# First block of a three-part transformer kernel: queries and keys projected early, all rotary turns on VectorE, scores of two heads in alternating halves of the array

## What is computed

```
p = u @ w_in                                  # u: normed, modulated x; (512, 2816)
q, k = rms_norm per head(q), (k);  q = rope_2d(q);  k = rope_2d(k)      # pairs within 16 + 16 columns
k_c, v_c = the same k and v columns of the context, k_c normed, not turned
o = softmax(q k_all^T / 8) v_all              # k_all, v_all: 256 context + 512 own tokens
attn = o * silu(p[za])
y = conv(a * sigmoid(g)), width 31, depthwise over 512 channels;  layer norm, silu, @ w_pw, * silu(p[zc])
h = x + gate * (concat(attn, y) @ w_out)
mod = silu(c) @ w_mod                         # the shifts, scales and gates of all blocks
```

## Time and profile before

| what | before |
|---|---|
| median of 3 runs (1949.14 to 1953.25) | 1950.08 us |
| the profiled execution: its time, its span | 1951.19 us, 1949.5 us |
| granted TensorE clock, mean of the profiled execution | 0.936 |
| TensorE busy | 1723.2 us, 88% of the span |
| VectorE busy | 1026.1 us, 53% |
| ScalarE busy | 653.0 us, 33% |
| GpSimd busy | 591.1 us, 30% |
| DMA | 187.14 MB, mean 96 GB/s |

### The profile page before, as it was taken

One profiled execution on the slowest core, in us unless ns is written; L12 is line 12 of the kernel. 1 busy time (PEld: TensorE's weight loads), 2 busy tenths in 40 slices (PEclk: granted clock), 3 DMA queues, 4 the chain that ended last, 5 costly groups with the idle time before them and its releaser, 6 DMA issues.

```text
span 1949.5 us, 23737 instructions
## 1 busy us (share of the span) xinstructions
PE 1723.2 (88%) x9380; PEld 1429.6 (73%) x9385; DVE 1026.1 (53%) x1305; ACT 653.0 (33%) x889; POOL 591.1 (30%) x515
## 2 busy tenths in 40 slices
PE   4997599788787789869999999899987799999997
PEld 3796489568786668748888787677766678888875
DVE  1568567575467675583333324655675743233344
ACT  4312255412122325243232212343444343332222
POOL 0005800262774000467887701222431300000012
PEclk8998799899788889989999999899997999999999
DMA  8553300143532000225565522221110222323221
GB/s 278 164 172 98 119 1 1 34 156 116 165 109 84 25 1 1 65 87 172 182 194 180 168 84 83 84 87 44 65 44 23 65 86 91 102 86 102 94 85 43
DMA packets 152521, 187.14 MB, mean 96 GB/s; under 512 B 6893, under 2 KB 117845, under 8 KB 152436
## 3 DMA queue, kind: packets, MB, share of 16 engines
q1 hardware_dynamic: 152436, 185.96, 29.6%
HBM read 183.85 MB, written 2.10 MB: 95 GB/s over the span
## 4 chain that ended last, share of the span: by engine, by line
PE 58%; POOL 16%; DVE 12%; issue 7%; ACT 4%; DMA 2%; POOLq 0%; SPq 0%; another core or an unknown queue 0%; DVEq 0%; ACTq 0%
PE ps L843 6%; PE ps L844 6%; PE ps L845 6%; POOL msum L627 5%; POOL mraw L620 5%; PE ps L1200 4%; PE ps L1201 4%; PE ps L1202 4%; PE ps L939 2%; PE ps L1234 2%; PE ps L863 2%; PE ps L1236 2%; PE ps L1235 2%; PE ps L865 2%; PE ps L866 2%
## 5 line engine op out<-in xcount | busy, mean ns | idle before, releaser
L1200 PE MATMUL ps<-uH,whi 128*128 128x512 f32 x704 | 278.6, 396 | 25.7 <-DVE uL L1841 25.4
L1202 PE MATMUL ps<-uH,wlo 128*128 128x512 f32 x704 | 276.5, 393 | 0.0
L1201 PE MATMUL ps<-uL,whi 128*128 128x512 f32 x704 | 276.1, 392 | 0.0
L1825 DVE TENSOR_TENSOR wlo<-wraw,whi 128x2048 fp32r<-128x2048 f32 x64 | 157.3, 2458 | 178.6 <-ACT whi L1372 178.4
L620 POOL TENSOR_TENSOR mraw<-mraw,cpad 128x1024 f32<-128x1024 f32 x64 | 129.1, 2017 | 380.8 <-PE ps L782 237.2
L1372 ACT ACTIVATE whi<-wraw 128x2048 fp32r<-128x2048 f32 x71 | 135.7, 1911 | 301.0 <-PE ps L845 268.0
L1200 PEld LDWEIGHTS ps<-uH,whi 128*128 128x128 f32 x704 | 133.7, 190 | 57.0 <-issue 20.8
L2344 DVE TENSOR_TENSOR wlo<-wraw,whi 128x2048 fp32r<-128x2048 f32 x22 | 51.2, 2327 | 206.8 <-ACT whi L1677 206.8
L1202 PEld LDWEIGHTS ps<-uH,wlo 128*128 128x128 f32 x704 | 133.4, 190 | 28.5
L1201 PEld LDWEIGHTS ps<-uL,whi 128*128 128x128 f32 x704 | 133.8, 190 | 27.4
L627 POOL TENSOR_TENSOR msum<-msum,mraw 128x512 f32<-128x512 f32 x96 | 150.8, 1571 | 7.5
(11 more groups left out here) (452 smaller groups left out, 3663.3 us busy)
## 6 DMA issues: line engine op xcount, KB each, us to landing
mraw<-in_w_mod_dram SPq DMA_DIRECT2D x104, 512.0 KB, 3.9
wraw<-in_w_gate_dram SPq DMA_DIRECT2D x22, 1024.0 KB, 5.3
wraw<-in_w_up_dram SPq DMA_DIRECT2D x22, 1024.0 KB, 5.5
wraw<-in_w_down_dram SPq DMA_DIRECT2D x16, 1024.0 KB, 5.0
wraw<-in_w_in_dram SPq DMA_DIRECT2D x11, 1024.0 KB, 5.5
wraw<-in_w_in_even_dram SPq DMA_DIRECT2D x9, 1024.0 KB, 6.6
mfirst<-in_w_mod_dram SPq DMA_DIRECT2D x16, 512.0 KB, 7.2
wraw<-in_w_in_odd_dram SPq DMA_DIRECT2D x16, 512.0 KB, 4.5
```

Of the source, the lines that this page charges most:

```text
L1200: mm(o, h_, uH[:, k], start=(k == 0), stop=False)
L1201: mm(o, h_, uL[:, k], start=False, stop=False)
L1202: last = mm(o, l_, uH[:, k], start=False, stop=(k == KT - 1))
L1825: V.tensor_tensor(wlo[:, n % 2, :], wraw[:, n % 2, :], whi[:, n % 2, :].bitcast(F32), ALU.subtract).then_inc(lo_done, 1)
```

## The change

The order of chunks becomes: first gate-and-value pair (0, 1), queries (2, 3), keys and values (4), second pair (5, 6), then z as before (`N_GLU, N_Q, N_KV = (0, 5), 2, 4`). VectorE turns keys (`turn_keys`, after chunk 4) and queries (`turn_query`, one token tile at each step n = 5 to 8), with fewer and larger operations for the keys; GpSimd's part and its zero fills go away, and GpSimd's sums for group 10 wait for the last convolution tap. Taps are given out by a table (55 before the attention, 69 in it). The columns of groups 6 to 8 are read at other places; all four ticks of group 8 belong to chunk 8, those of group 9 to chunk 9, two of each in the chunk's middle, and group 8 gets a bank of its own. Keys are transposed in the middles of chunks 8 and 9, queries in the middle of chunk 10 and behind it. `kH` and `kL` get their own memory and no zeros: scores of an even and an odd head are computed together, matmuls alternating between rows 0 to 63 and 64 to 127, into two pairs of banks. The order of items changes with that (`item`, `column`). The splits of chunk 12 move into the attention. In the second block two operations of VectorE (`dsa_max`, `dsa_move`) get the widths that TensorE and ScalarE already use for the same items.

```diff
-N_GLU, N_Q, N_KV, N_ZA, N_ZC, N_PW, N_WO = 0, 4, 6, 7, 9, 11, 13
+N_GLU, N_Q, N_KV, N_ZA, N_ZC, N_PW, N_WO = (0, 5), 2, 4, 7, 9, 11, 13
...
+TAPS_AT = {1: 5, 2: 7, 3: 10, 5: 6, 6: 5, 7: 7, 8: 7, 9: 8}
+assert sum(TAPS_AT[n] for n in TAPS_AT if n < 7) <= 2 * TAPS
+TURN_AT = {2: 4, 4: 5, 6: 6, 8: 7, 9: 8, 10: 9}
+COLUMNS_AT = {5: 6, 7: 7, 8: 8}
+QUERY_AT = {5: 0, 6: 1, 7: 2, 8: 3}
...
+def item(i):
+    return 2 * (i // 8) + i % 2, i // 2 % 4
+
+
+def column(i):
+    h, qt = item(i)
+    return 4 * h + qt
...
-        gt, = overlay([("gt", [P, 4, 256], F32)])
+        gt, kH, kL = overlay([("gt", [P, 4, 256], F32), ("kH", [P, 2, 768], F32R), ("kL", [P, 2, 768], F32R)])
...
         def ticks_of(n):
-            if n in (N_PW - 1, N_PW):
-                return (0, 1, 2, 3) if n == N_PW - 1 else ()
-            return (2 * (n % 2), 2 * (n % 2) + 1) if n < NC1 - 1 else ()
+            if n in (8, 9):
+                return (0, 1, 2, 3)
+            return (2 * (n % 2), 2 * (n % 2) + 1) if n < 8 or 12 <= n < NC1 - 1 else ()
 
         def group_of(n):
-            return 4 + n // 2
+            return n if n in (8, 9) else 4 + n // 2
...
+            return acc[:, g, :] if g < 4 else (X[:, 2, :] if g == 8 else modp)
...
+            pool.wait_ge(conv_rd, 4)
...
-                if kp == 0 and g >= 5:
-                    pe.wait_ge(mod_rd, g)
+                if kp == 0 and g >= 5 and g != 8:
+                    pe.wait_ge(mod_rd, min(g, 8))
...
+            def key_job(j):
+                pe.wait_ge(rope_rd, 1)
+                pe.wait_ge(ctx_read, 1)
+                if j:
+                    pe.wait_ge(qk_lo, 1)
+                for c in range(6):
+                    last = tr(key_bank[:, c * P:c * P + P], kdup[:, c, j].rearrange("p e d -> p (e d)"), ident[:])
+                last.then_inc(qkT, 1)
+
+            def query_job(j):
+                if j == 0:
+                    pe.wait_ge(rope_v, TT)
+                    pe.wait_ge(qk_lo, 2)
+                if j >= 2:
+                    pe.wait_ge(mod_rd, 7 + j)
+                for tt in range(TT):
+                    last = tr(oTp[j][:, tt * P:tt * P + P], qtok[:, tt, j * P:j * P + P], ident[:])
+                last.then_inc(qkT, 1)
+
+            def middle(n):
+                def steps():
+                    if n in (8, 9):
+                        tick(n, 0)
+                        tick(n, 1)
+                        key_job(n - 8)
+                    if n == 10:
+                        query_job(0)
+                        query_job(1)
+                return steps
...
+            query_job(2)
+            query_job(3)
             acc_gone(pe, N_PW - 1)
-            acc_gone(pe, N_PW - 2)
-
-            def scores(i):
-                h, qt = i // 4, i % 4
-                if i >= 2:
-                    pe.wait_ge(p_rd, i - 1)
-                ql = slice(qt * P, qt * P + P)
+
+            def scores(p):
+                h, qt = item(2 * p)
+                if qt == 0:
+                    pe.wait_ge(qk_lo, 3 + h // 2)
+                if p >= 1:
+                    pe.wait_ge(p_rd, 2 * p)
+                ql, half = slice(qt * P, qt * P + P), [slice(0, HD), slice(HD, P)]
                 for c0, c1 in ((0, 512), (512, 768)):
-                    o = pair[i % 2][:, c0:c1]
-                    q_h, q_l = qH[:, h // 2, ql], qL[:, h // 2, ql]
-                    k_h, k_l = kH[:, h % 2, h // 4, c0:c1], kL[:, h % 2, h // 4, c0:c1]
-                    mm(o, q_h, k_h, start=True, stop=False)
-                    mm(o, q_h, k_l, start=False, stop=False)
-                    last = mm(o, q_l, k_h, start=False, stop=True)
-                last.then_inc(s_rd, 1)
+                    for e in range(2):
+                        mm(pair[e][:, c0:c1], qH[half[e], h // 2, ql], kH[half[e], h // 4, c0:c1], start=True, stop=False)
+                    for e in range(2):
+                        mm(pair[e][:, c0:c1], qH[half[e], h // 2, ql], kL[half[e], h // 4, c0:c1], start=False, stop=False)
+                    for e in range(2):
+                        last = mm(pair[e][:, c0:c1], qL[half[e], h // 2, ql], kH[half[e], h // 4, c0:c1],
+                                  start=False, stop=True)
+                        if c1 == 768:
+                            last.then_inc(s_rd, 1)
...
+                if i % 2 == 0 and i + 2 < NS:
+                    scores(i // 2 + 1)
...
+                if i == 2:
+                    split_high(N_PW + 1)
...
+            def turn_query(tt):
+                v = qtok[:, tt].rearrange("p (h d) -> p h d", d=HD)
+                dve.wait_ge(u_lo, U_UC + 8)
+                link(V.tensor_tensor(v, v, qrs[:, tt * NH:tt * NH + NH].unsqueeze(2).to_broadcast([P, NH, HD]), ALU.mult))
+                link(V.tensor_tensor(v, v, qkw[:, 0:1, :].to_broadcast([P, NH, HD]), ALU.mult))
+                v = qtok[:, tt].rearrange("p (h a z f) -> p h a z f", a=2, z=2, f=16)
+                one, two = v[:, :, :, 0, :], v[:, :, :, 1, :]
+                tm = [tmp[:, i // 2, 256 * (i % 2):256 * (i % 2) + 256].rearrange("p (h a f) -> p h a f", a=2, f=16)
+                      for i in range(4)]
+                cs, sn = [ropet[:, i, tt].rearrange("p (o a f) -> p o a f", o=1, a=2)
+                          .to_broadcast([P, NH, 2, 16]) for i in range(2)]
+                V.tensor_tensor(tm[0], one, cs, ALU.mult)
+                V.tensor_tensor(tm[1], two, sn, ALU.mult)
+                V.tensor_tensor(tm[2], one, sn, ALU.mult)
+                link(V.tensor_tensor(tm[3], two, cs, ALU.mult))
+                V.tensor_tensor(one, tm[0], tm[1], ALU.subtract)
+                V.tensor_tensor(two, tm[2], tm[3], ALU.add).then_inc(rope_v, 1)
+                dve.wait_ge(rope_v, tt + 1)
+
+            def query_low(j):
+                dve.wait_ge(qk_hi, j + 3)
+                V.tensor_tensor(qL[:, j], oTp[j], qH[:, j].bitcast(F32), ALU.subtract).then_inc(qk_lo, 1)
+
+            def turn_keys():
+                kv = kvt[:, :, 0:P].rearrange("p t (h d) -> p t h d", d=HD)
+                link(V.tensor_tensor(kv, kv, qrs[:, 32:44].rearrange("p (t h) -> p t h", h=2).unsqueeze(3)
+                                     .to_broadcast([P, 6, 2, HD]), ALU.mult))
+                link(V.tensor_tensor(kv, kv, qkw[:, 1, :].unsqueeze(1).unsqueeze(1).to_broadcast([P, 6, 2, HD]), ALU.mult))
+                cs, sn = [ropet[:, i].rearrange("p t (a f) -> p t a f", a=2) for i in range(2)]
+                for h in range(2):
+                    v = kv[:, 2:6, h].rearrange("p t (a z f) -> p t a z f", a=2, z=2)
+                    one, two = v[:, :, :, 0, :], v[:, :, :, 1, :]
+                    tm = [tmp[:, h, P * i:P * i + P].rearrange("p (t a f) -> p t a f", t=TT, a=2) for i in range(4)]
+                    V.tensor_tensor(tm[0], one, cs, ALU.mult)
+                    V.tensor_tensor(tm[1], two, sn, ALU.mult)
+                    V.tensor_tensor(tm[2], one, sn, ALU.mult)
+                    link(V.tensor_tensor(tm[3], two, cs, ALU.mult))
+                    for e in range(2):
+                        d = kdup[:, 2:6, h, e, :].rearrange("p t (a z f) -> p t a z f", a=2, z=2)
+                        V.tensor_tensor(d[:, :, :, 0, :], tm[0], tm[1], ALU.subtract)
+                        V.tensor_tensor(d[:, :, :, 1, :], tm[2], tm[3], ALU.add)
+                for e in range(2):
+                    last = V.tensor_copy(kdup[:, 0:CT, :, e, :], kv[:, 0:CT])
+                last.then_inc(rope_rd, 1)
...
+            tapped = 0
             for n in range(N_PW):
+                if n in (8, 9):
+                    dve.wait_ge(qk_hi, n - 7)
+                    V.tensor_tensor(kL[:, n - 8], key_bank, kH[:, n - 8].bitcast(F32), ALU.subtract).then_inc(qk_lo, 1)
+                if n == 10:
+                    group_columns(9)
+                    query_low(0)
+                    query_low(1)
...
+                if n == N_KV:
                     dve.wait_ge(qrs_rd, 1)
...
+                    dve.wait_ge(u_lo, U_UC + 8)
+                    turn_keys()
+                if n in QUERY_AT:
+                    turn_query(QUERY_AT[n])
+                if n in TAPS_AT:
+                    if n == min(TAPS_AT):
                         acc_gone(dve, 1)
-                    for q in range(TG * (n - N_Q), TG * (n - N_Q) + TG):
+                    if n == N_GLU[1] + 2:
+                        acc_gone(dve, N_GLU[1] + 1)
+                    for q in range(tapped, tapped + TAPS_AT[n]):
                         tap(q)
 
-                        if n % 2 and q % TG == TG // 2:
-                            group_columns(3 + (n + 1) // 2)
-
+                        if n in COLUMNS_AT and q == tapped + (0 if n == 5 else TAPS_AT[n] // 2):
+                            group_columns(COLUMNS_AT[n])
+                    tapped += TAPS_AT[n]
...
+            q = tapped
             maxima(0)
             maxima(1)
-            for i in range(NS):
-                if i + 2 < NS:
```

(46 more changed lines are left out.)

161 lines of the change are left out of this document (45 added, 116 removed).

## The result

The changed kernel takes 1907.38 us (median of 4 runs, 1904.41 to 1910.87), against 1951.66 for the kernel before beside it (4 runs): a ratio of 0.977, with a 95% interval of 0.9745 to 0.9798. Predicted were 1901.5 and a range of 1892 to 1920. Of the gain, 44.3 us by these medians, 48.6 had been forecast. The profiled execution took 1904.41 us, with a span of 1902.7 and a mean clock of 0.948, so 46.8 us less span than before. TensorE is busy for 1704.8 us (90%), VectorE for 1024.6 (54%), GpSimd for 517.7 (27%).

What follows compares the result with a forecast made beforehand. TensorE was taken as the bound, with some 35 us of gaps before the attention and none in it. Terms -41.2 - 4.4 - 3.0 = -48.6 us gave 1901.5 against the median of 1950.1; range 1892 to 1920.

Steps and rivals of the forecast that it cites:

- Term 1: Work up to the attention: the first `turn` comes at 210.1 us against 251.3, -41.2 us.
- the 208 to 214: Sign that the forecast is right: the attention's first `turn` comes at 208 to 214 us.
- the 0.7 us stall: At tick (7,0), end of chunk 6: TensorE waits for VectorE's columns of group 6, booked at 0.7 us.
- Rival (a): Before the attention: loads or VectorE's turns stop the chunks, costing 5 to 14 us, kernel about 1911; chance 0.17.
- Term 2: First block's attention, first turn to layer norm's mean: 90.8 us against 95.2, -4.4 us.
- S: TensorE's time for one double score, two items' scores together, in the attention: 1.5 us against 2.30 before.
- Rival (b): The attention doesn't gain, VectorE and ScalarE bound it: each pair near 6.0 us, kernel 1906 to 1908; chance 0.14.
- Term 3: Behind the attention: TensorE's 3.5 us wait for GpSimd's group 10 sum goes, the mean waits 0.5; -3.0 us.
- Rivals (c) to (e): Later stages tighten too, about 1892 us, 0.07; lower TensorE clock, 1978, 0.03; gap before attention only moved, 1922 to 1935, 0.04.

## Why the prediction was right, and where not

**Term 1, -41.2, measured -37.0.** The failed step is the first one: "Chunks 0 to 6 hold the same matmuls in another order and had no long gap, so I let chunk 7 start at 152.3 as now". The order was not neutral. The turn of group 4 stands in chunk 2, now a token chunk, and its middle by the code is a quarter of it; ScalarE's `copy_group(4)` stands behind three context tiles, which moved too. Wait and clock cost 4.9 us, shown by the edit that takes them away. The rest of the step is small: 0.65 us of the 4.7 by which chunk 7 came later stood at the tick of 82 us already (82.01 for 81.36), and without the wait the new order takes 68.9 us from that tick to tick (7,0) where the old one took 69.9. The wait would have been found by following each `turn_group` of the new table to its copy, as I did for VectorE's columns.
From there on the steps hold: 52.3 for 52.0 up to chunk 10's end, 5.0 for 5.1 from there to the first turn. The first turn at 214.3 is just outside the 208 to 214 that I gave as a sign. A `turn_query` took 3.7 us for 3.9, `turn_keys` 6.0 for 7, and the keys' scaling began 0.3 us behind the reciprocal, where I had put 1.5 for the root and a table load: the load (1.28 us at 137.1) ran beside VectorE's reductions. The chain for group 6's columns was 23.3 us from chunk 4's end (131.5) instead of 25.3, so the 0.7 us stall did not come; with the columns at 154.8 and the tick at 155.95 it is tight as worked out. The loads were never late. Rival (a) is out. How the 37 us divide between the order of the chunks, VectorE's turns and the transposes in the middles is argued from the waits, not shown: only the queries' 5.7 us were measured by themselves.

**Term 2, -4.4, measured -6.1.** The parts were S = 1.5, which is 1.24 (the 256-column pairs leave every 0.12 us, not 0.20 as the earlier trace rows suggested), and 5.6 a pair, which is 5.53; the rest is in the fixed parts. I named VectorE alone as the bound, and had TensorE's own work at 5.22 with S = 1.5. It is 5.34 with S = 1.24: the term that I mis-sized is the two turns and two values, 4.1 for 3.72. The turn ahead of the scores takes 0.75 for 0.58 and the one ahead of values 0.66; the values behind the scores take 1.39 for 1.28. The 0.1 us that I read from the first pair's 0.34 in the earlier trace rows as a drain is none: full-height scores took 0.32 there as well (284.70 to 285.02 in the kernel before); the change stands ahead of the scores, in the 0.75. So the gain came from S alone, and TensorE's own work and VectorE's each decide in some pairs. That 5.6 came so near is in part luck, for it is the mean of two kinds of periods, 5.33 to 5.43 and 5.58 to 5.91. No run has the old full-height scores in the new order, so the share of the half-height matmuls in the 6.1 us is worked out, not measured. My 88 us for VectorE should have been 88.7. Rival (b) is out.

**Term 3, -3.0, measured -3.8 and -0.7** in two profiles of the same kernel: not settled beyond "between 0 and -4". GpSimd's 3.5 us wait became 2.2 and 0.5, but a wait of up to 5.1 for a low part grew in its place (3.3 in the first profile, 1.2 before), as VectorE's angles fall beside GpSimd's group 11 (without them beside it, 0.4 us). The widths alone left the ratio at 0.9998, 0 within 2.5 us.

**Rivals (c) to (e).** The clock stays at 0.98 to 1.00, the last query turn ends at 191.1 us, 12 us ahead of its transposes, and no stage gave more than 6.1 us beside term 1.

What stays open: why the time from the mean to GpSimd's last fill varies between 176 and 182 us over kernels that are the same there, and so where gains of 2 or 3 us ahead of it go.

## What to carry to other kernels

When the order of chunks changes, follow every small step that rides on them (turns, copies, columns) to its new producer, even where the matmuls are the same; a wait of 3.5 us cost 1.4 more through the clock behind it. Of two waits in a row the earlier one, 11.1 us, was worth nothing while the later one, for another engine, stood. Work taken from GpSimd can pay even where GpSimd is in time (5.7 us here), through what it did to VectorE's operations on SBUF beside it; idle time of GpSimd can be what keeps VectorE fast. When matmuls of half and of full height alternate, add the change between them to TensorE's sum: here some 0.4 us a pair.

## What the runs showed of the hardware

- A VectorE operation of 128x512 with both inputs in SBUF took 0.62 us alone and 1.8 beside GpSimd's sums, a 128x128 one with one input 0.23 and 1.3; one with an input in PSUM took 0.62 in both cases. VectorE's 128x2048 split kept its 2.28 us, and GpSimd's operation beside it took 2.73 instead of 1.18.
- Half-height matmuls on alternate halves leave in pairs: 512 columns every 0.23 us, 256 columns every 0.12. In head-after-head order twelve of them took 1.84 us instead of 1.24. Six transposes took 0.75 us to the start of half-height matmuls, against 0.58 to full-height ones; the step back took 0.20 us instead of 0.12 (249.16 to 249.36).
- Behind an idle time of 3.5 us TensorE ran at 0.50 of its clock for 3.1 us, the lower of its two levels (1.2 GHz).
